# First gather of an expert stage without its last two row tiles: the missing rows selected on chip by one-hot products, first blocks in another order

## The reference, cut to what matters

```python
h2 = x * (1 + sc2) + sh2
scores = sigmoid(h2 @ w_router)
sel = scores + router_bias
# the best group of 4 experts, then the best 2 experts in it
gate = normalized scores of the two
for e in range(16):
    he = silu(h2 @ w_e_gate[e]) * (h2 @ w_e_up[e])
    y = y + gate[e] * (he @ w_e_down[e])
x = layer_norm(ALPHA * x + (1 + g2) * y)
```

## Time and profile before

| What | Value |
|---|---|
| median of three runs | 1038.35 us (1035.55 to 1040.6) |
| the profiled execution's own time | 1047.34 us |
| its span, first to last instruction | 1045.5 us |
| PE busy | 1003.7 us, 96% of the span |
| DVE, ACT, POOL busy | 548.0, 198.9, 254.4 us |
| mean granted TensorE clock | 0.983 of full speed |
| moved by DMA | 214.98 MB, 206 GB/s |

### The profile page before, as it was taken

How to read it: one execution, slowest core, us unless ns; L and a number is a source line. 1 busy time by engine, 2 the same in 40 slices (tenths; PEclk the granted TensorE clock), 3 DMA queues, 4 the chain that set the end, 5 groups by cost and what they waited for, 6 DMA issues and landing times.

```text
span 1045.5 us, 23523 instructions
## 1 busy us (share of the span) xinstructions
PE 1003.7 (96%) x9535; PEld 722.8 (69%) x9535; DVE 548.0 (52%) x1381; ACT 198.9 (19%) x474; POOL 254.4 (24%) x284
## 2 busy tenths in 40 slices
PE   6999999999999999899999999999999999999995
PEld 5777777567776767567777764577876678667764
DVE  2122999983367888967446715587133121011137
ACT  2110112113232333232211100111111111111104
POOL 0100003634121223132435610001212122421123
PEclk9999999999999999999999999977999999999998
DMA  9964744644505215114081338243899999899995
GB/s 300 327 135 138 220 163 151 214 165 150 203 11 174 69 51 178 40 30 124 12 213 49 121 116 337 71 191 111 326 390 404 351 396 411 323 392 396 394 267 113
DMA packets 94003, 214.98 MB, mean 206 GB/s; under 512 B 23572, under 2 KB 48407, under 8 KB 89797
## 3 DMA queue, kind: packets, MB, share of 16 engines
q1 hardware_dynamic: 78388, 186.20, 50.0%
q0 software_dynamic: 6672, 19.67, 6.4%
q10 hardware_dynamic: 8841, 7.64, 2.6%
HBM read 201.12 MB, written 16.92 MB: 209 GB/s over the span
## 4 chain that ended last, share of the span: by engine, by line
PE 86%; DVE 6%; DMA 3%; issue 3%; ACT 1%; ACTq 0%; SPq 0%; POOL 0%; POOLq 0%; DVEq 0%
PE banks L2121 37%; PE banks L2540 15%; PE banks L2562 8%; PE banks L2135 6%; PE banks L2155 5%; PE banks L2125 3%; DMA arena<-in_w_ada 2%; PE banks L2243 1%; DMA arena<-expert_rows 1%; PE banks L2549 1%; PE banks L2522 1%; PE banks L2173 1%; PE banks L2371 1%; PE banks L2412 1%; DVE arena L1460 1%
## 5 line engine op out<-in xcount | busy, mean ns | idle before, releaser
L2121 PE MATMUL banks<-arena 128*128 128x288 f32 (+6 forms) x1774 | 427.9, 396 | 4.6 <-PE banks L2243 1.7
L2121 PEld LDWEIGHTS banks<-arena 128*128 128x128 f32 (+1 forms) x1774 | 318.0, 191 | 107.4 <-issue 30.2
L2540 PE MATMUL banks<-arena 128*32 128x256 f32 x3136 | 186.3, 380 | 1.8 <-issue 1.8
L2540 PEld LDWEIGHTS banks<-arena 128*32 128x32 f32 x3136 | 129.1, 109 | 47.3 <-issue 4.1
L2049 DVE TENSOR_TENSOR arena<-arena,banks 128x128 f32<-128x128 f32 x49 | 14.1, 288 | 220.0 <-ACT arena L1354 219.7
L2562 PE MATMUL banks<-arena 128*32 128x256 f32 x1568 | 101.8, 379 | 2.2 <-issue 1.9
L1052 POOL DMA_INDIRECT expert_rows<-arena,ints x44 | 43.0, 977 | 195.4 <-ACT arena L1365 191.3
L994 POOL TENSOR_SCALAR arena<-arena 128x288 f32<-128x288 f32 x46 | 45.4, 987 | 168.1 <-ACT arena L1276 101.8
L1431 DVE SCALAR_TENSOR_TENSOR arena<-arena 128x512 f32<-128x512 f32 x120 | 81.9, 742 | 0.0
L2562 PEld LDWEIGHTS banks<-arena 128*32 128x32 f32 x1568 | 61.4, 109 | 23.2 <-issue 6.7
L2135 PE MATMUL banks<-arena 128*128 128x288 f32 x256 | 65.1, 409 | 1.0 <-DVEq L1449 1.0
(11 more groups left out here) (325 smaller groups left out, 1026.6 us busy)
## 6 DMA issues: line engine op xcount, KB each, us to landing
arena<-in_w_e_gate SPq DMA_DIRECT2D x16, 2048.0 KB
arena<-in_w_e_up SPq DMA_DIRECT2D x16, 2048.0 KB
arena<-in_w_e_down SPq DMA_DIRECT2D x16, 2048.0 KB
arena<-in_w_ada SPq DMA_DIRECT2D x8, 2048.0 KB, 9.7
arena<-in_w_in SPq DMA_DIRECT2D x8, 2048.0 KB, 9.8
arena<-in_w_ada SPq DMA_DIRECT2D x8, 1024.0 KB, 11.6
arena<-in_x_prompt SPq DMA_DIRECT2D x8, 512.0 KB, 7.2
arena<-in_w_in SPq DMA_DIRECT2D x14, 256.0 KB, 8.8
```

The lines of the kernel that those rows point to most:

```text
L2121: last = pe.matmul(out, a, b, start=k == 0, stop=k == len(pairs_) - 1)
L2540: last = pe.matmul(out, HG[:, g % 2, k, a:a + BLK], both_weights(i, k, c), start=k == 0, stop=k == KT - 1)
```

## The change

The new kernel lets `gather(0)` fetch only those of the first 128 rows whose token lies in tiles 0, 1 or 2. Tiles 3 and 4 are still in SBUF (`H2`), and their rows are brought to their places, and transposed, by one product per 128 features with a one-hot matrix. The gathered rows are transposed by a product with `FOUND`, an identity in which the rows that were not gathered are zero. All three sources are summed in banks 3 and 4, which two products with a zero operand clear first. `near_rows` makes one matrix of 128 columns (96 places for expert 0, 32 for expert 1) where it made two. The list of tokens is complete after tile 2, so `first_list` comes before `rt` of tile 4; POOL waits for three stores. Fillers are moved, and the order of the first four blocks and of what lies among them is written out by hand on PE and DVE. `places_up` (the second half of `list_up`, unchanged) is now called later on DVE.

```diff
@@ -287,8 +287,8 @@
         plan += [("wo", t, 1)]
-    plan += [("wo", 4, 0), ("wo", 4, 1), ("near", 1), ("h2T", 3, 0), ("h2T", 3, 1), ("cum", 2), ("rt", 3), ("h2T", 4, 0), ("h2T", 4, 1), ("rt", 4)]
-    plan += [("cum", 3), ("near", 2), ("cum", 4), ("cnt",), ("near", 3), ("near", 4)]
+    plan += [("wo", 4, 0), ("wo", 4, 1), ("near", 1), ("h2T", 3, 0), ("h2T", 3, 1), ("cum", 2), ("rt", 3), ("h2T", 4, 0), ("h2T", 4, 1)]
+    plan += [("near", 2), ("rt", 4), ("cum", 3), ("cum", 4), ("cnt",)]
     return plan
@@ -459,8 +459,8 @@
-    HOT, SUMM = V(A_HOT, 2, 2, P), V(A_HOT + 4 * P, 3, NE)
-    AT01, OK01, NEAR = V(A_HOT + 4 * P + 48, 2), V(A_HOT + 4 * P + 50, 2), V(A_HOT + 4 * P + 52, 1)
+    HOT, SUMM = V(A_HOT, 2, P), V(A_HOT + 4 * P, 3, NE)
+    AT01, NEAR, FOUND = V(A_HOT + 4 * P + 48, 2), V(A_HOT + 4 * P + 50, 2), V(A_HOT + 2 * P, P)
     RSTDT, NMRT = sm(0, 5), sm(5, 5)
@@ -536,6 +536,7 @@
     tile_behind = {max(4 * g - 2, 3): g for g in range(1, TILES)}
+    near_places = {0: (0, BLK * NB_AT[0]), 1: (BLK * NB_AT[0], TS)}
@@ -1020,10 +1021,12 @@
         pool.wait_ge(ev("first_list"), 1)
-        pool.wait_ge(ev("h2_out0"), 16 * 3)
-        pool.wait_ge(ev("h2_out1"), 16 * 2)
+        pool.wait_ge(ev("h2_out0"), 16 * 2)
+        pool.wait_ge(ev("h2_out1"), 16)
         def gather(g):
             if g == 1:
+                pool.wait_ge(ev("h2_out0"), 16 * 3)
+                pool.wait_ge(ev("h2_out1"), 16 * 2)
                 pool.wait_ge(ev("list_int"), 1)
@@ -1347,22 +1350,29 @@
+        def rows_out(d):
+            if d >= SENT:
+                return
+            act.wait_ge(ev("dn_full"), d + 1)
+            if d >= YRS:
+                act.wait_ge(*stored(d - YRS))
+            if d == 0:
+                act.wait_ge(ev("weights_up"), 1)
+            act.activation(YR[:, yr_of(d), :], banks[6 + d % 2][:, 0:256], ACT.Copy, scale=WBLK[:, d:d + 1]).then_inc(ev("yo_up"), 1)
         rows_up(0, 0)
...
             act.activation(HEB[:, b % 3, :], banks[b % 3][:, gate_half(turn_of[b])], ACT.Silu).then_inc(ev("he_silu"), 1)
+            if b == 3:
+                rows_out(0)
             if b in tile_behind:
...
                 rows_up(g, g % 2)
-            d = b - 2
-            if 0 <= d < SENT:
-                act.wait_ge(ev("dn_full"), d + 1)
-                if d >= YRS:
-                    act.wait_ge(*stored(d - YRS))
-                if d == 0:
-                    act.wait_ge(ev("weights_up"), 1)
-                act.activation(YR[:, yr_of(d), :], banks[6 + d % 2][:, 0:256], ACT.Copy, scale=WBLK[:, d:d + 1]).then_inc(ev("yo_up"), 1)
+            if b > 2:
+                rows_out(b - 2)
         nov = act.value_load(ints[0:1, I_NOV:I_NOV + 1], min_val=0, max_val=NOV)
@@ -1592,14 +1602,14 @@
             dve.sem_inc(at.free(("cum", t)), 1)
-            place = SLM[0:n, t, 0:2]
-            done(stt(AT01[0:n], place, -float(TS), con[0:n, K_BASE:K_BASE + 2], ALU.add, ALU.add))
-            link(stt(OK01[0:n], place, float(BLK * BLOCKS_OF[0]), MSK[0:n, t, 0:2], ALU.is_le, ALU.mult))
-            link(tt_(AT01[0:n], AT01[0:n], OK01[0:n], ALU.mult))
+            link(stt(AT01[0:n], SLM[0:n, t, 0:2], -float(TS), con[0:n, K_BASE:K_BASE + 2], ALU.add, ALU.add))
+            link(tt_(AT01[0:n], AT01[0:n], MSK[0:n, t, 0:2], ALU.mult))
             if t >= 2:
                 dve.wait_ge(*at.full(("near", t - 2)))
-            tt_(HOT[0:n, t % 2], AT01[0:n].unsqueeze(2).broadcast_to([n, 2, TS]), RCON[0:n, R_LO:].unsqueeze(1).broadcast_to([n, 2, TS]),
-                ALU.is_equal).then_inc(ev("near_hot"), 1)
+            for e in range(2):
+                a, b = near_places[e]
+                hot = tt_(HOT[0:n, t % 2, a:b], AT01[0:n, e:e + 1].broadcast_to([n, b - a]), RCON[0:n, R_LO + a:R_LO + b], ALU.is_equal)
+                hot.then_inc(ev("near_hot"), 1)
@@ -1945,14 +1955,14 @@
                 if t == 0:
-                    link(dve.tensor_copy(NEAR, ps[:, 0:1]))
-                elif t < 4:
-                    link(tt_(NEAR, NEAR, ps[:, 0:1], ALU.add))
+                    link(dve.tensor_copy(NEAR, ps[:, 0:2]))
                 else:
-                    link(tt_(NEAR, NEAR, ps[:, 0:1], ALU.add))
-                    link(dve.tensor_copy(ints[:, I_L:I_L + 1], NEAR))
+                    link(tt_(NEAR, NEAR, ps[:, 0:2], ALU.add))
+                dve.sem_inc(at.free(key), 1)
+                if t == 2:
+                    link(dve.tensor_copy(ints[:, I_L:I_L + 1], NEAR[:, 1:2]))
                     dve.sem_inc(ev("first_list"), 1)
-                dve.sem_inc(at.free(key), 1)
+                    ts(FOUND, ident, NEAR[:, 0:1], None, ALU.mult).then_inc(ev("found_up"), 1)
             if kind == "rt":
@@ -2038,15 +2049,31 @@
-        for b in range(NBLK + 2):
-            if b == 1:
-                weigh_rows()
-                list_up()
-            if b == 2:
-                weights_up()
+        def hidden_up(b):
+            dve.wait_ge(ev("he_silu"), b + 1)
+            tt_(HEB[:, b % 3, :], HEB[:, b % 3, :], banks[b % 3][:, up_half(turn_of[b])], ALU.mult).then_inc(ev("he_ready"), 1)
+        def flipped_up(b):
+            dve.wait_ge(ev("flip_full"), b + 1)
+            dve.tensor_copy(HETB[:, b % 2], banks[5][:, 0:P].rearrange("p (c t) -> p c t", t=BLK)).then_inc(ev("het_up"), 1)
+        hidden_up(0)
+        hidden_up(1)
+        weigh_rows()
+        list_up()
+        flipped_up(0)
+        hidden_up(2)
+        places_up()
+        weights_up()
+        flipped_up(1)
+        further_tiles()
+        spread_up()
+        flipped_up(2)
+        hidden_up(3)
+        rows_up(1, 1)
+        for b in range(4, NBLK + 2):
             if b < NBLK:
-                dve.wait_ge(ev("he_silu"), b + 1)
-                tt_(HEB[:, b % 3, :], HEB[:, b % 3, :], banks[b % 3][:, up_half(turn_of[b])], ALU.mult).then_inc(ev("he_ready"), 1)
+                hidden_up(b)
                 if 6 <= b < 6 + 2 * NT:
@@ -2059,11 +2086,8 @@
                 rows_up(g, g % 2)
-            if 1 <= b <= NBLK:
-                dve.wait_ge(ev("flip_full"), b)
-                dve.tensor_copy(HETB[:, (b - 1) % 2], banks[5][:, 0:P].rearrange("p (c t) -> p c t", t=BLK)).then_inc(ev("het_up"), 1)
-            if b == 2:
-                spread_up()
+            if b <= NBLK:
+                flipped_up(b - 1)
@@ -2172,7 +2196,7 @@
-        fillers = {("h2T", 4, 0): (3, 256), ("cum", 3): (1, 256), ("near", 3): (1, 256)}
+        fillers = {("h2T", 4, 0): (4, 256), ("cum", 3): (1, 256), ("cum", 4): (4, 256)}
@@ -2482,8 +2506,8 @@
                 n = rows_of(t)
-                pe.wait_ge(ev("near_hot"), t + 1)
-                last = group(ps[:, 0:1], [(HOT[0:n, t % 2, e, :], con[0:n, K_TOK + t:K_TOK + t + 1]) for e in range(2)])
+                pe.wait_ge(ev("near_hot"), 2 * t + 2)
+                last = group(ps[:, 0:2], [(HOT[0:n, t % 2, :], con[0:n, K_ONE:K_TOK + t + 1:K_TOK + t - K_ONE])])
             if not split:
@@ -2520,6 +2544,23 @@
                 last = pe.transpose(banks[3 + k // 4][:, (k % 4) * P:(k % 4) * P + P], G[:, z, k:D:KT], ident)
+            last.then_inc(ev("gt_full"), 1)
+        def first_rows():
+            row_of = lambda k: banks[3 + k // 4][:, (k % 4) * P:(k % 4) * P + P]
+            nought = slice(32, 64)
+            for bank in (3, 4):
+                pe.matmul(banks[bank], con[nought, K_E8:K_E8 + P], con[nought, 0:512], start=True, stop=False)
+            for t in (3, 4):
+                n = rows_of(t)
+                pe.wait_ge(ev("near_hot"), 2 * t + 2)
+                for k in range(KT):
+                    pe.matmul(row_of(k), H2[0:n, t % 2, k:D:KT], HOT[0:n, t % 2, :], start=False, stop=False)
+            pe.wait_ge(ev("found_up"), 1)
+            pe.wait_ge(ev("rows_gathered0"), 16)
+            for k in range(KT):
+                last = pe.matmul(row_of(k), G[:, 0, k:D:KT], FOUND, start=False, stop=k % 4 == 3)
             last.then_inc(ev("gt_full"), 1)
@@ -2563,27 +2604,31 @@
-        unread(9, 256)
-        gathered(0, 0, 16)
         unread(2, 256)
-        for b in range(NBLK + 2):
+        first_rows()
+        unread(2, 256)
+        for b in range(3):
+            hidden(b)
+        row_list()
+        hidden_flip(0)
+        hidden(3)
+        row_weights()
+        hidden_flip(1)
+        down(0)
+        spread()
+        hidden_flip(2)
+        down(1)
+        pe.wait_ge(ev("weights_up"), 1)
+        gathered(1, 1, 16)
+        for b in range(4, NBLK + 2):
             if b < NBLK:
                 hidden(b)
-            if b == 1:
-                row_list()
-            if b == 2:
-                row_weights()
             if b in tile_behind:
                 g = tile_behind[b]
-                if g == 1:
-                    pe.wait_ge(ev("weights_up"), 1)
                 gathered(g, g % 2, 16 * (g // 2 + 1))
-            if 1 <= b <= NBLK:
+            if b <= NBLK:
                 hidden_flip(b - 1)
-            if b == 2:
-                spread()
```

(7 more changed lines are left out.)

## The result

The new kernel takes 1046.45 us (median of 20 runs, 1042.85 to 1050.33), the kernel before 1039.36 us (20 runs, 1033.85 to 1044.08). The ratio is 1.0076 (1.0063 to 1.009): slower by 7.1 us, where 2.1 were forecast. The profiled execution of the new kernel has a span of 1044.8 us and a time of its own of 1046.61 us.

What follows compares the result with a forecast made beforehand. PE, holding 86% of the chain, was taken as the bound. Front +1.9, wait for copies +1.0 and clock -0.8 gave +2.1 us on a median of 1038.35: 1040.5 us, range 1034.5 to 1046.5.

Steps and rivals of the forecast that it cites:

- The front up to the end of `cnt`: PE, from the router product of tile 4 through fillers and narrow products: `cnt` ends at 708.3.
- Fillers and clearing products: PE behind `cnt`, at full clock: two fillers 0.86 us, two clearing products of 512 columns 1.72 us.
- The 24 products: PE before the first block: 0.25 us each, 6.0 us (5.2 to 6.5), in place of eight transposes.
- a product costs over 0.3 at full clock: Sign of being wrong, for the 24 products on PE; the forecast took 0.25 us each.
- The clock: PE's front: full clock returns between 706.2 and 713.9, taken as 710.0, losing 0.85 us.
- if the clock returns by 706: Sign of being wrong, in PE's front; the earliest return forecast was 706.2.
- clock stays down through all one-hot products: Slower rival, front from 708.3: all runs at half clock, +8.2 us, 1046.5 us; chance 0.15.
- no change within 0.5%: Outcome for the whole kernel's time: a change within 5.2 us either way; chance 0.68.
- The first blocks: PE from the first block to block 4: +1.0 us waiting for copies, -0.8 us for the clock.
- the fall of the clock there: Narrow products among the first blocks: the fall may stay, go or come twice, +1.7 to -1.7 us; taken -0.8.
- What was hidden: Gather, DVE steps and SP loads beside PE: no added time; the gather has 8 us of slack.
- Sum: Whole kernel: +1.9 us to the first block, +1.0 for copies, -0.8 for the clock, +2.1 us.

Runs made afterwards that it cites:

- e6: The kernel before with only the new order of the first blocks, old front kept; ratio 1.0025 to the kernel before.
- e12: The new kernel without its two clearing products, the first product of each bank starting the sum; 1044.92 us, ratio 1.0051 to the kernel before.
- e10: The kernel before with the eight transposes of every gathered tile made products with the identity, same stepped weights; 1072.23 us, ratio 1.0324.
- e8: New front with features in another layout (unstepped weights), no clearing products, old order of blocks; ratio 1.0025 to the kernel before.
- e11: The new kernel with unstepped weights in its 24 products, run and profiled once more; 1040.41 us, ratio 1.0027 to the kernel before.
- e2: The new kernel with unstepped weights in its 24 one-hot products, first tile's rows permuted; 1040.62 us, ratio 1.0017 to the kernel before.
- e5: The new kernel's front with the old order of the first blocks; ratio 1.0043 to the kernel before.
- e1: The kernel before, unchanged, timed against itself; 1039.39 us against 1038.28, ratio 1.0002.
- e9: The new kernel with one-hot matrices as weights in six wide products, then transposes; no clearing products, old block order; 1037.25 us, ratio 0.9992.
- e7: The kernel before with features loaded in another layout, so its transposes need no step; ratio 1.0025 to the kernel before.

## Why the prediction was wrong, step by step

**The front up to the end of `cnt`.** Forecast: 708.3, which is 19.0 behind `wo` (689.32). Measured: 708.84 - 692.47 = 16.4. The narrow and filler products there ran partly at full clock, which came back once before `h2T` 4 was done; the forecast had taken all their prices at half clock from the earlier trace rows. This hid 2.6 us of the loss that follows. In all nine profiles with the new front `cnt` ends 16.3 to 17.5 behind `wo`. The same return of the clock stands in e6, with the old front, and gave nothing there: its nine fillers began 18.7 behind `wo` as before, as PE waited.

**Fillers and clearing products.** Forecast 0.86 and 1.72; measured 1.06 and 1.91; without the clearing products 1.6 were won (e12). Right. So was the end: 1.2 from the last product to the first block, against 1.22 (724.18 to 725.40).

**The 24 products: the step that failed.** "I take 0.25: 6.0 us (5.2 to 6.5)." They took 12.36. The upper bound was drawn from the stepped transposes of the earlier trace rows, 0.136 each, twice; it assumed that a product is two transposes' worth of loads. The runs show that it isn't: the load of a transpose takes 193 ns, that of a product with the same weights 335 ns (e10), and they follow each other at 0.136 and at 0.25. Unstepped and at full clock a product costs 0.2475 (e8, e11); that this is the 0.25 of the forecast is luck, as the forecast meant stepped ones and took a middle of two bounds. The sum was off by 6.4 us in this one term. The sentence that said "a product costs over 0.3 at full clock" makes me wrong names it.

The Trainium skill (TensorE: Matmul & The Clock Gate, LDWEIGHTS) has a load depend on the number of weight columns alone, as an estimate by it 0.107 us, beside the running products; by it the 24 would cost 5.1, again an estimate. The runs disagree for float32 weights with a step: with the same columns a product at full clock costs 0.50 with the step (e10) and 0.2475 without (e11), and its loads last 335 and 192 ns. The measurement decides.

**The clock.** Forecast: back between 706 and 714, taken 710, at a cost of 0.85. It was back at 707.4 already and fell again at 714. `wo` ended 3.15 later than in the profile that the forecast counts from, so on its axis the return is at 704.2, ahead of the earliest end: the first sign of being wrong, "if the clock returns by 706", came true. The rival "clock stays down through all one-hot products" gave 1046.5, which is nearly the time measured, by a mechanism that is not the one at work: with the clock full (e10, e12) the products were as slow. It had a chance of 0.15, and slower altogether 0.19, against 0.68 for no change within 0.5%; that 1046.45 lies just below the upper end, 1046.5, which is that rival's value, is luck. At one and the same mean granted clock, 0.982, eight runs of the new kernel took 1045.46 to 1048.33 us, and eleven of the kernel before, 1038.08 to 1041.59. So the scatter of each kernel goes with the clock, and the difference between them is there at an equal mean clock too. An equal mean doesn't part the step from the clock, though: e2, without the step, took 1045.67 at 0.982.

**The first blocks.** The wait before block 4 was forecast at 1.0 (0.7 to 1.2) and is 0.8; the fall of the clock there, of which the prediction took half (-0.8), stayed, once, from 745 to 748. Sum forecast +0.2, measured +0.8; by e5 and e6 the order alone costs 1.0 to 1.1 us up to block 4.

**What was hidden stayed hidden.** The gather was issued 12.3 behind `wo`, forecast 12.0; it was 19.5 before. PE didn't wait for it in any run. No wait stands in front of `row_list` or `spread`. The earlier loads of the third expert bought nothing that can be told: 1.2 us less behind block 4 in the one pair of spans.

**Sum.** Forecast +1.9 to the first block. To it come 6.4 from the products and 0.4 from fillers and clearing, and from it go 0.85 of clock cost that didn't occur and the 2.6 ahead of `cnt`: +5.2, as measured. With the 0.8 of the blocks that is 6.0 of the 7.1 us.

**What stays open.** The last microsecond; the ratios of e5 and e6 allow that it belongs to the order of the blocks. Before the end of `wo` the clock is at half for 3.4 us in the three profiles of before, e1 and e10, and for 6.8 to 13.7 us in all eleven others, by a further fall near 87 us or, in e12, a longer one at 433, in stages that no edit touches; `wo` ends up to 4 us later in them. Eleven of eleven against none of three doesn't look like chance; but e12 has it at another place than the rest, e6 has it with the old front, and e9, which has it too, takes no longer than the kernel before. No run was made to settle it.

## What to carry to other kernels

Before a transpose with stepped weights is turned into a product, price the product by itself: in float32 it cost 0.46 to 0.52 us here for 128 features with a step of eight, at either clock, against 0.136 for the transpose and, at full clock, 0.25 for a product with unstepped weights. Let the stepped array be what passes through as data, or permute by wide products first and transpose afterwards (e9, which won nothing either). A bound made of rows of another kind of operation (here: transposes for products) is no bound; where the trace has no row of the operation, the upper end has to leave room for it.

## What the runs showed of the hardware that I had not expected

- At full clock the weight load of a plain float32 product with a step of eight elements takes 335 ns (e10) and they follow each other at 0.25 us; unstepped 192 ns and 0.124 (e11); in a transpose 193 ns and 0.136 stepped, 140 ns and 0.128 unstepped (e7). Reading the weights with a step is nearly free for a transpose and doubles a product. At half clock unstepped loads of a product take 333 ns too (e2), so the duration of a load alone doesn't give the step away. The loads of e11, e2 and e7:

```profile
L2563 PEld LDWEIGHTS banks<-arena x16: 186/192/193, 719.5 to 721.2; 128*128 128x128 f32 x16
...
L2563 PEld LDWEIGHTS banks<-arena x16: 286/333/333, 718.5 to 721.6; 128*128 128x128 f32 x16
...
L2522 PEld LDWEIGHTS banks<-arena x104: 138/140/146, 717.2 to 1004.8; 128*128 128x128 f32 x104
```

- Such a product hardly notices the clock (0.46 to 0.50 in e10 and 0.48 in e12 at full, 0.51 for the last eight of the new kernel at half), while an unstepped one does (0.2475 and 0.464). A slow stretch at a granted clock of 0.50 is therefore no proof that the clock is the cause.
- The clock fell at 714 in the new kernel while PE was busy without a gap; in e12 it stayed full through the same 16 products. What decides between the two these traces don't tell.
